# A three-layer transformer on one core: slabs split in two parts, another order of loading at the start, queries and keys left whole in the last block

## The reference

```python
# first_block, layer 0: even mixer, then squared-ReLU MLP (4096 wide)
h = rmsnorm(x, norm_mix[0])
qa, ka, va, fa, qb, kb, vb = split(h @ w_in)            # 8 + 8 heads of 64, fa: 8 forget gates
log_f = log_sigmoid(fa + b_forget)
o_a = softmax(qa ka^T / 8 + cumsum(log_f)_q - cumsum(log_f)_k, causal) va
o_b = softmax(qb kb^T / 8 + rel_bias, chunked) vb
x = x + concat(o_a, o_b) @ w_out
x = x + square(relu(rmsnorm(x) @ w_up)) @ w_down
# first_block, layer 1: odd mixer (stick-breaking heads; MLA heads with rotary), then the same MLP
# second_block: hybrid mixer, then SwiGLU (2816 wide)
dq, dk, nq, ... = split(u @ w_in); dq, dk, nq, k_sel, k_win = rotary(...)
y_a = (softmax(dq1 dk1^T) - lam * softmax(dq2 dk2^T)) dv
k_cmp, v_cmp = silu(blocks @ w1) @ w2                   # compressed keys and values, 31 of them
o_c = softmax(nq k_cmp^T) v_cmp; o_s = selected blocks; o_w = window
y_b = g_c * o_c + g_s * o_s + g_w * o_w                 # g: sigmoid gates
x = x + (sigmoid(m_a) * y_a @ w_a + sigmoid(m_b) * y_b @ w_b) @ w_out
x = x + (silu(u @ w_gate) * (u @ w_up)) @ w_down
return rms_norm(x)
```

## Time and profile before

| | |
|---|---|
| median of 3 runs | 2235.84 us (2232.83 to 2241.22) |
| profiled execution | 2241.18 us, span 2239.4 us |
| busy: PE, PEld | 2098.6 us (94%), 1677.9 us (75%) |
| busy: DVE, ACT, POOL | 1071.9 us, 891.8 us, 786.7 us |
| rounding of a slab (L1002, 323 times) | mean 1059 ns |
| subtraction of a slab (L420, 322 recorded) | mean 2436 ns |
| slabs loaded | 323 of 512 KB, median 3.3 us from issue to landing |
| mean granted clock of TensorE | 0.973 |

### The profile page before, as it was taken

One profiled execution on the slowest core, in us unless ns is written; L12 is line 12 of the kernel. 1 busy time (PEld: TensorE's weight loads), 2 busy tenths in 40 slices (PEclk: granted clock), 3 DMA queues, 4 the chain that ended last, 5 costly groups with the idle time before them and its releaser, 6 DMA issues.

```text
span 2239.4 us, 28086 instructions
## 1 busy us (share of the span) xinstructions
PE 2098.6 (94%) x10360; PEld 1677.9 (75%) x10360; DVE 1071.9 (48%) x1326; ACT 891.8 (40%) x1468; POOL 786.7 (35%) x327
## 2 busy tenths in 40 slices
PE   6999889999999987899999998888989999999997
PEld 4877668888887665678888886666767878888885
DVE  5454563313256677563323365776554554313235
ACT  4455443323233654442323346555454223222222
POOL 2322134444443310044444443341112434444443
PEclk9999989999999999999999999998899999999998
DMA  3122112223222200022232231221001222223223
GB/s 138 62 80 67 47 66 94 94 97 101 94 94 94 66 29 29 19 94 94 97 101 94 94 102 59 94 76 48 29 29 46 96 85 94 95 94 99 99 94 103
DMA packets 50659, 178.44 MB, mean 80 GB/s; under 512 B 5488, under 2 KB 5752, under 8 KB 50560
## 3 DMA queue, kind: packets, MB, share of 16 engines
q1 hardware_dynamic: 46512, 169.37, 22.9%
q10 hardware_dynamic: 4048, 7.69, 1.0%
HBM read 174.92 MB, written 2.12 MB: 79 GB/s over the span
## 4 chain that ended last, share of the span: by engine, by line
issue 54%; PE 29%; POOL 12%; DVE 3%; ACT 1%; POOLq 1%; DVEq 0%
POOL w_lo L420 12%; PE gemm_banks L443 9%; PE gemm_banks L444 8%; PE gemm_banks L445 8%; PE score_banks L892 1%; PE out_banks L935 1%; PE score_banks L903 1%; DVE turned L2048 1%; PE score_banks L875 0%; POOLq L416 0%; ACT tmp L1069 0%; DVE top L1671 0%; DVE share L2060 0%; PE gemm_banks L852 0%; DVE x L1512 0%
## 5 line engine op out<-in xcount | busy, mean ns | idle before, releaser
L420 POOL TENSOR_TENSOR w_lo<-raw,w_hi 128x1024 fp32r<-128x1024 f32 x322 | 784.1, 2436 | 1431.6 <-ACT w_hi L1002 1431.3
L1002 ACT ACTIVATE w_hi<-raw 128x1024 fp32r<-128x1024 f32 x323 | 342.0, 1059 | 889.8 <-PE gemm_banks L445 870.2
L443 PE MATMUL gemm_banks<-h_hi,w_hi 128*128 128x512 f32 (+2 forms) x1520 | 622.5, 410 | 34.2 <-DVE h_lo L1504 16.2
L445 PE MATMUL gemm_banks<-h_hi,w_lo 128*128 128x512 f32 (+2 forms) x1520 | 599.3, 394 | 0.0
L444 PE MATMUL gemm_banks<-h_lo,w_hi 128*128 128x512 f32 (+2 forms) x1520 | 598.9, 394 | 0.0
L443 PEld LDWEIGHTS gemm_banks<-h_hi,w_hi 128*128 128x128 f32 (+2 forms) x1520 | 287.2, 189 | 114.1 <-issue 42.2
L443 PE MATMUL gemm_banks<-u_hi,w_hi 128*128 128x512 f32 x848 | 332.6, 392 | 13.6 <-POOL w_lo L420 9.6
L445 PEld LDWEIGHTS gemm_banks<-h_hi,w_lo 128*128 128x128 f32 (+2 forms) x1520 | 286.9, 189 | 65.3 <-issue 2.0
L444 PE MATMUL gemm_banks<-u_lo,w_hi 128*128 128x512 f32 x848 | 331.7, 391 | 0.0
L444 PEld LDWEIGHTS gemm_banks<-h_lo,w_hi 128*128 128x128 f32 (+2 forms) x1520 | 287.8, 189 | 58.4 <-issue 4.0
L445 PE MATMUL gemm_banks<-u_hi,w_lo 128*128 128x512 f32 x848 | 331.5, 391 | 0.0
(11 more groups left out here) (323 smaller groups left out, 2090.1 us busy)
## 6 DMA issues: line engine op xcount, KB each, us to landing
raw<-slabs SPq DMA_DIRECT2D x323, 512.0 KB, 3.3
x<-x_t ACTq DMA_DIRECT2D x2, 1024.0 KB, 9.6
t_raw<-rel_rows ACTq DMA_DIRECT2D x4, 512.0 KB, 4.0
y_t<-x ACTq DMA_DIRECT2D x8, 256.0 KB, 2.1
consts<-consts_packed ACTq DMA_DIRECT2D x1, 516.5 KB, 5.0
cos<-pos ACTq DMA_DIRECT2D x2, 256.0 KB, 10.2
params<-params_packed ACTq DMA_DIRECT2D x1, 179.5 KB, 10.7
VT<-lam ACTq DMA_DIRECT2D x1, 128.0 KB, 9.6
```

What stands on the lines that cost most here:

```text
L420: pool.tensor_tensor(w_lo[:, j, :], raw[:, j, :], w_hi[:, j, :].bitcast(F32), ALU.subtract).then_inc(slab_split, 1)
L443: pe.matmul(out, high, rhs_hi, start=first, stop=False)
L445: return pe.matmul(out, low, rhs_hi, start=False, stop=last)
L1002: act.activation(w_hi[:, m % 2, :], raw[:, m % 2, :], ACT.Copy).then_inc(slab_hi, 1)
```

## The change

It has four parts. The slabs are rounded, subtracted and waited for in two parts of 512 columns (four tiles), and `slab_hi` and `slab_split` count parts. At the start, `x` comes as eight transfers on two queues, the parameters first on ScalarE's and slab 0 first on SyncE's; the weights of the forget gates move from slab 0 into the parameters, are split by VectorE, and their matmuls are done tile by tile together with those of the first values; the gates' chain comes behind the evacuation of the first values, and partly behind the queries. The rotary tables are made beside the down product of the first quarter of layer 0's MLP. In the last block the rotated queries and keys stay fp32 (`QT`, `KTT`, `k_sel`, `k_win`, `kcmp`), and their scores are one fp32 matmul for each head.

```diff
@@ SyncE
-            for j in range(2):
-                sp.dma_start(raw[:, j, :], slabs[j]).then_inc(raw_landed[j], 16)
+            sp.dma_start(raw[:, 0, :], slabs[0]).then_inc(raw_landed[0], 16)
+            for j in (0, 2, 4, 6):
+                sp.dma_start(x[:, j, :], x_in[j * P:(j + 1) * P, :]).then_inc(x_landed[j], 16)
+            sp.dma_start(consts[:, :], consts_in).then_inc(small_landed, 16)
+            sp.dma_start(raw[:, 1, :], slabs[1]).then_inc(raw_landed[1], 16)
+            ... (lambda, relative biases, positions)
@@ GpSimd
-                    pool.wait_ge(slab_hi, i * 2 + (j + 1))
-                    pool.tensor_tensor(w_lo[:, j, :], raw[:, j, :], w_hi[:, j, :].bitcast(F32),
+                    for k in range(2):
+                        part = slice(k * (SLAB // 2), (k + 1) * (SLAB // 2))
+                        pool.wait_ge(slab_hi, i * 4 + (2 * j + k + 1))
+                        pool.tensor_tensor(w_lo[:, j, part], raw[:, j, part], w_hi[:, j, part].bitcast(F32),
+                                           ALU.subtract).then_inc(slab_split, 1)
@@ TensorE, gemm_slab (likewise in the other products)
-                pe.wait_ge(slab_split, c.slab.at(1))
                 for kt in range(tiles):
+                    if kt % 4 == 0:
+                        pe.wait_ge(slab_split, c.slab.at(1 + kt // 4, 2))
@@ TensorE, start
-            gemm_slab(h_hi, h_lo, width=8, fresh=1)
-            pe.wait_ge(small_landed, 32)
+            pe.wait_ge(forget_split, 2)
+            for kt in range(KT):
+                pe.wait_ge(act_lo, c.lo.at(kt + 1))
+                for n, (w, h) in enumerate(((wf_hi, h_hi), (wf_hi, h_lo), (wf_lo, h_hi))):
+                    last = pe.matmul(OB[0:8, 0, :], w[:, kt, :], h[:, kt, :], start=(kt == 0 and n == 0),
+                                     stop=(kt == KT - 1 and n == 2), skip_group_check=True)
+                ...
+                last = product(G[:, c.gemm.slot, :], kt, P, h_hi[:, kt, :], h_lo[:, kt, :], kt == 0, kt == KT - 1)
@@ TensorE, e_scores
-                parts = ((q_hi, keys[0]), (q_hi, keys[1]), (q_lo, keys[0]))
-                for n, (q, k) in enumerate(parts):
-                    for head in range(2):
-                        rows = slice(HEAD * head, HEAD * (head + 1))
-                        last = pe.matmul(SC[:, 2 * (s % 2) + head, 0:w], q[rows, p % 2, i * P:w], k[rows, 0:w],
-                                         start=False, stop=n == 2, skip_group_check=True)
+                for head in range(2):
+                    rows = slice(HEAD * head, HEAD * (head + 1))
+                    pe.matmul(SC[:, 2 * (s % 2) + head, 0:w], QT[rows, p % 2, i * P:w], keys[rows, 0:w], start=False,
+                              stop=True, skip_group_check=True).then_inc(scored, 1)
@@ ScalarE
-                act.activation(w_hi[:, m % 2, :], raw[:, m % 2, :], ACT.Copy).then_inc(slab_hi, 1)
+                for k in range(2):
+                    part = slice(k * (SLAB // 2), (k + 1) * (SLAB // 2))
+                    act.activation(w_hi[:, m % 2, part], raw[:, m % 2, part], ACT.Copy).then_inc(slab_hi, 1)
...
+            act.dma_start(params[:, :], params_in).then_inc(params_landed, 16)
+            for j in (1, 3, 5, 7):
+                act.dma_start(x[:, j, :], x_in[j * P:(j + 1) * P, :]).then_inc(x_landed[j], 16)
             split(0)
-            split(1)
-            act.wait_ge(small_landed, 32)
+            act.wait_ge(params_landed, 16)
             for j in range(KT):
-                act.wait_ge(x_landed[j // 4], 16)
+                act.wait_ge(x_landed[j], 16)
                 gained(j, gains_of("mix0"))
                 square(x[:, j, :])
+                if j == 5:
+                    split(1)
...
-            project_out(gains_of("mlp0"), rotary_table)
-            mlp(gains_of("mix1"))
+            project_out(gains_of("mlp0"))
+            mlp(gains_of("mix1"), beside=rotary_table)
...
-                elif name in SPLIT:
-                    ...
-                    act.activation(dst, tmp[:, 2, :], ACT.Copy).then_inc(qk_hi, 1)
@@ VectorE, start
+            evacuated(0, KT)
+            dve.wait_ge(forget_full, 1)
+            dve.tensor_tensor(tmp[0:8, 2, :], OB[0:8, 0, :], rstd[0:8, :], ALU.mult).then_inc(forget_in, 1)
+            evacuated(KT, 2 * KT)
+            ... (the gates' chain)
+            low_parts(KT, 2 * KT)
+            evacuated(2 * KT, 3 * KT)
+            low_parts(2 * KT, 3 * KT)
+            ... (the three copies of the relative biases)
@@ VectorE, last block
-                    dve.tensor_tensor(lo[at], tmp[:, 2, :], hi[at].bitcast(F32), ALU.subtract).then_inc(qk_split, 1)
...
-                    dve.tensor_tensor(tmp[:, 2, :], tmp[:, 2, :], tmp[:, 3, :], ALU.add).then_inc(rope_ready, 1)
+                    dve.tensor_tensor(dst, tmp[:, 2, :], tmp[:, 3, :], ALU.add).then_inc(rope_ready, 1)
```

More of the change, by code:

```diff
@@ L210 @@
 ROTATED = ("q", "k", "kc", "ks", "kw", "nq")
-SPLIT = ("q", "k", "ks", "kw", "nq")
 def plan_e():
@@ L1166, in _, with project_out @@
             c.hi.now += KT
-            def project_out(gains, beside=lambda j: None, more=None):
+            def project_out(gains, more=None):
                 for j in range(KT):
@@ L1189, in square_relu, with mlp @@
                 link(act.activation(tmp[:, 2 + s, :], tmp[:, s, :], ACT.Square))
-            def mlp(gains, more=None):
+            def mlp(gains, more=None, beside=lambda j: None):
                 def up(first):
@@ L1733, in split_u, with mlp @@
                 c.hi.now += 1
-            def mlp(gains, more=False):
+            def mlp(gains, more=False, beside=lambda j: None):
                 mean(D, rstd)
-                with c.loop(dve, 3, slab=16, gemm=16, hi=8, lo=8):
+                for j in range(8):
+                    split_u(j, relu())
+                add_out(beside=beside, squares=False)
+                c.slab.now += 8
+                with c.loop(dve, 2, slab=16, gemm=16, hi=8, lo=8):
                     for j in range(8):
```

228 lines of the change are left out of this document (108 added, 120 removed).

## The result

The changed kernel takes 2181.44 us (median of six runs, 2179.58 to 2186.11), the kernel before 2237.19 on the same chip (2228.70 to 2241.22): ratio 0.9758, 95% interval 0.9737 to 0.978, 55.7 us less. The forecast was 2193 in a range of 2172 to 2220: the direction and the range held, and the gain was forecast at 43.0. The two profiled executions are 60.1 apart (2241.18 and 2181.09; spans 2239.4 and 2179.3), because that of before is at the top of its runs; so a table made from the traces shows some 4 us more than the medians do.

The account below looks back on a forecast made before the run. TensorE was taken as full in the feed-forward stretches, so only idle time and slow clock elsewhere could be gained. The terms summed to -43.0 us, from 2235.84 to 2193, range 2172 to 2220.

Parts of the forecast that it names:

- The start, -13.5: Up to the first scores: earlier loads and a moved gates' chain start them at 39.5, not 53.00; bounds -11 and -16.
- The rotary tables, -15.8: Moved from layer 0's output product to the down product: 10.2 us of waits and 5.6 of slow clock go.
- Rival C: Rotary tables don't fit the down product and their 10 us of waiting return: 2203; 7 in 100.
- Parts where TensorE waits for slabs, -3.2 and -8.7: Half slabs shorten slab waits: -3.2 at two seams, -8.7 in the last block's attention and at the compression weights.
- The merge, -1: In the merge, VectorE's m_hi stands behind a GpSimd subtraction; a block half as long gives -1 us.
- ScalarE's cost in the stick-breaking steps, +2.2: Two roundings per slab cost ScalarE more where TensorE waits for its exponentials: +2.2 us, bounds 0 and +5.
- rival B: GpSimd's parts free VectorE, so idle and slow clock in the last block shrink: another -18, 2175; 10 in 100.
- fp32 scores, +4.4: Last block, 48 steps: one fp32 pair of score matmuls replaces three fp32r pairs, +4.4 us; other end +30.
- rival A: fp32 matmuls on row halves run one after the other: +25.6 more, 2218; 15 in 100.
- The compressed scores: Last block: they lose eight of twelve matmuls, the four left cost up to twice: -2.4 us, bounds 0 and -4.
- The removed splits, -4, and -1 of slow clock: Last block: fourteen splits of queries and keys go, mostly beside TensorE: -4 and -1 us, bounds 0 and -20.
- Rival D: A wait in mid-slab makes TensorE drain, so a weight load of 0.19 us shows: 61 us slower, 2254; 3 in 100.

Follow-up runs that it names:

- ScalarE whole: The changed kernel with ScalarE rounding a slab in one instruction of 1024 columns again, GpSimd still subtracting in two halves: 2184.53 us, ratio 0.9779.
- The quarters: The changed kernel with GpSimd subtracting a slab in four instructions of 256 columns: 2177.18 us, ratio 0.9756.
- the unsplit queries and keys alone: The kernel before with only the last block's queries and keys left unsplit: 2225.30 us, ratio 0.9955.
- quarters and the new order: The changed kernel with GpSimd subtracting in quarters and another order of VectorE's work in the start: 2174.04 us, ratio 0.972.

## Why the prediction was right or wrong

**The start, -13.5: too much; -10.2 by its marks, some -8 with what follows.** The loads and the first half are near what I forecast: first matmul at 8.78 (8.1), parameters landed 4.3 after their issue. The first nine matmuls ran 0.43 apart, and the gates and first values ended at 21.47 (20.9). The step that failed is "the gates' chain of 6.6 us ... with rstd at 24.5 it runs from 28.2 to 35". It ran from 29.28 to 40.06, because it now lies beside GpSimd's subtractions:

```profile
29.28 1.49 DVE L1686 TENSOR_SCALAR tmp<-tmp,params 8x512 f32<-8x512 f32 x1
30.80 1.66 DVE L1687 TENSOR_TENSOR tmp<-tmp 8x512 f32<-8x512 f32 x1
...
35.34 1.40 DVE L1693 TENSOR_SCALAR turned<-fox_t 8x512 f32<-8x512 f32 x1
36.75 1.68 DVE L1694 SCALAR_TENSOR_TENSOR turned<-tmp,fox_t 8x512 f32<-8x512 f32 x1
38.47 1.67 DVE L1699 TENSOR_SCALAR fox_b<-turned,consts 128x512 fp32r<-128x512 f32 x4
40.06 0.68 DVE L1627 TENSOR_TENSOR q_lo<-tmp,q_hi 128x512 fp32r<-128x512 f32 x1
```

The first pair of lines 1693 and 1694, which started at 34.19 and 34.62, took 0.42 and 0.68; this one, behind the start of two subtractions at 34.63, took 1.40 and 1.68. Before, no subtraction runs between 28.25 and 39.32, and the chain lies in that gap. I had read such blocks in the rotary tables and in the earlier trace rows, had even allowed 0.7 to 2.4 for `k_lo`, and took the chain's length from a place where it met no subtraction. I also gained the 2 us of slow clock of the earlier trace rows and did not see that the new wait makes a stretch of its own (1.7 to 2.1).

**The rotary tables, -15.8: right in kind, near in size (14.2 beside whole slabs, 11.0 beside parts).** The waits and the slow stretches are gone; what is left of the place is one wait of 0.28. The chain there took 9.2 us (345.93 to 355.09) and not 7.3, again for GpSimd, and the spare of 2.2 at the bank carried it. Rival C did not come.

**Parts where TensorE waits for slabs, -3.2 and -8.7: right.** Each seam's wait went from 2.99 to 1.48, and the waits for slabs in the last block from 12.1 to 5.8, which is 6.3 and inside the bounds of 4 to 12; putting whole slabs back costs 9.5 in that stage. Behind layer 1's seam 1.7 us of slow clock went too, which I had not priced. A half costs 1.30 and not 1.20, which hardly matters. The merge, -1, gave nothing. TensorE waits there for `m_lo`, 4.79 before and 4.74 after. Before, the two operations of VectorE ahead of it are these:

```profile
1811.82 0.69 DVE L2109 TENSOR_TENSOR tmp<-tmp 128x512 f32<-128x512 f32 x1
...
1812.55 2.45 DVE L2110 TENSOR_SCALAR m_hi<-tmp 128x512 fp32r<-128x512 f32 x1
```

After, they stand beside two halves in a row (1752.34 to 1755.27), and each half holds one of them:

```profile
1752.43 1.72 DVE L2112 TENSOR_TENSOR tmp<-tmp 128x512 f32<-128x512 f32 x1
...
1754.18 1.37 DVE L2113 TENSOR_SCALAR m_hi<-tmp 128x512 fp32r<-128x512 f32 x1
```

That is 3.14 and 3.09 in sum. A half shortens the block of one operation; a chain of VectorE's that is as long as the whole subtraction meets both halves.

**ScalarE's cost in the stick-breaking steps, +2.2, and nothing for VectorE there: with the last block the largest miss.** Layer 1's attention gained 8.5, where the forecast had +0.6 with the seam; putting whole slabs back takes 5 to 7 of it away. ScalarE's price is not to be seen: with ScalarE whole the stage takes the same 225.5. (Its busy time over the kernel went up by 29 us for the roundings, 342 to 371, and not by 64: of two in a row the second begins before the first is recorded as ended.) What I left out is VectorE, which I had as rival B with 10 in 100, and looked for in the last block only. It acts in layer 1 too, where I had put nothing for it. The rule of the Trainium skill's page "SBUF — State Buffer", section "SBUF: two separate sides", of a lock held for the whole instruction, agrees with the pair of 2.33 and 0.81, and the blocks should have been priced in every stage in which VectorE's operations on SBUF lie beside subtractions (line 1693 above, with one input from SBUF, was held up as well: 1.40 against 0.42). The quarters agree too: the average of `u_lo` falls from 1.83 (whole, before) to 1.26 to 1.00.

**fp32 scores, +4.4: right, +3.8 measured; rival A falls.** A pair of 512 columns, and the product behind it:

```profile
1575.23 1.13 PE L911 MATMUL score_banks<-k_win,QT 64*128 64x512 f32 x4
1576.29 0.50 PE L449 MATMUL gemm_banks<-h_hi,w_hi 128*128 128x512 f32 x1
```

Start to start it is 1.06 with the change of tile form, against 0.89 for three fp32r pairs; one after the other it would be over 1.7. By widths of 128 to 512 the differences are -0.06, +0.08, +0.13 and +0.17, twelve times each. The compressed scores went from 1.37 to 0.81 to 0.91 at the full clock, which gives -2.0 over four of them, and 2.56 to 1.72 at half, for a forecast of -2.4.

**The removed splits, -4, and -1 of slow clock: the second is the mis-sized term.** Putting them back costs 7 in the stage, by 3 to 6 more lost to the clock and a wait for `VT` of 4.0 in place of 2.8. With the scores' +3.8 and the compressed scores' -2, the splits themselves are worth some 9. In the sum I priced the waits and hardly what a wait leads to, although had shown 2 to 3 us lost behind each of the long ones and the clock of 0.93 stood in the earlier trace rows.

**Rival D** is gone: in the long product a slab still takes 5.44 us, and a wait in the middle or between slabs shows nothing.

```profile
503.84 0.39 PE L451 MATMUL gemm_banks<-h_hi,w_lo 128*128 128x512 f32 x1
504.06 0.39 PE L449 MATMUL gemm_banks<-h_hi,w_hi 128*128 128x512 f32 x1
...
509.28 0.39 PE L451 MATMUL gemm_banks<-h_hi,w_lo 128*128 128x512 f32 x1
509.50 0.39 PE L449 MATMUL gemm_banks<-h_hi,w_hi 128*128 128x512 f32 x1
```

Of what I had said would prove me wrong one thing came: the last block's attention as I measured it, 400 us before, had to end between 383 and 395, and it lost 21 and not 5 to 17. So the total was right within its range partly by luck, by two errors of opposite sign: the start gained 3 to 5 too little, and the two attentions 18 too much for the forecast. 2181.44 lies at the edge of what I had called the likeliest case (2180 to 2206), and nearer to rival B's 2175, to which I had given 10 in 100, than to 2193.

## What to carry to other kernels

When one engine's long instructions make another wait, cut them, and look for the gain wherever the second engine is on the path, not only where the first one's result is awaited; here half of the parts' gain lay elsewhere. Take the length of a moved chain from beside its new neighbours, not from its old place. And price a wait of TensorE with the slow stretch behind it: of the 60 us between the two traces, 26 were clock.

## What the runs showed of the hardware

The same wait can be followed by very different lengths at 1.2 GHz. The longest wait of the last block (3.55 to 3.71 us in every kernel, for `turned`) is followed in 16 us by these rows, before and after:

```profile
1558.78:1574.78 16.00, 15.92 (x71) 12.46 (x71) 7.09 (x17) 4.92 (x14) 0.00 (x0) 0.58 0.01 4
```

```profile
1510.47:1526.47 16.00, 15.43 (x94) 10.60 (x95) 8.78 (x21) 7.38 (x18) 2.31 (x2) 0.89 0.01 3
```

A clock of 0.58 is 13.4 us at half speed, one of 0.89 is 3.5. Of the twelve other profiles four have 0.89 too and eight 0.79 to 0.82, those with whole slabs among both; so the 0.58 is likely that one execution's and not the kernel's, and with it some 3 to 5 us of what the two traces differ by in the last block. The next wait (2.87 to 3.10 us) had 0.68 before and between 0.71 and 1.00 in the others: no slow stretch at all with ScalarE whole, with the unsplit queries and keys alone, and with quarters and the new order. Behind the first scores a wait of 2.2 left the clock at 1.00, and one of 1.8 in another kernel had 0.61 over 4 us. So a wait's length alone doesn't tell what follows it, and single stages move by a few us for this reason. What decides it these runs don't show.

GpSimd's subtraction has a small fixed price: 2.40 whole, 1.26 at least and 1.30 in the median for a half, 0.74 in the median for a quarter. Some halves are recorded with up to 2.43. Two halves of 1.30 in place of 2.40 make 0.2 us a slab, 64 us of the 88 by which GpSimd's busy time grew; the rest is in the longer ones. In one place these wait for VectorE: the two halves that start at 34.63, 0.01 us behind an operation of VectorE of 0.68, take 3.26 together in place of 2.6. That the others do so too is not shown.
